# Two heads at a time through TensorE in the attention of the last two mixers

## The reference, cut to what matters

```python
def stick_breaking_attention(q, k, v):          # (heads 8, S = 256, dh = 64)
    z = q @ k.T * dh ** -0.5
    earlier = key_pos < query_pos
    log_keep = where(earlier, log_sigmoid(-z), 0.0)
    log_stick = cumsum(log_keep, over keys, reverse) - log_keep
    w = where(earlier, exp(log_sigmoid(z) + log_stick), 0.0)
    return w @ v
```

## Time and profile before

| what | value |
|---|---|
| median of 3 runs | 2064.53 us (2064.52 to 2066.67) |
| span of the profiled execution | 2064.4 us |
| TensorE matmul busy | 2025.7 us, 98% |
| VectorE busy | 1374.4 us, 67% |
| ScalarE busy | 1105.1 us, 54% |
| mean granted TensorE clock | 0.996 of full speed |

### The profile page before, as it was taken

How to read it: one execution, slowest core, us unless ns; L and a number is a source line. 1 busy time by engine, 2 the same in 40 slices (tenths; PEclk the granted TensorE clock), 3 DMA queues, 4 the chain that set the end, 5 groups by cost and what they waited for, 6 DMA issues and landing times.

```text
span 2064.4 us, 28014 instructions
## 1 busy us (share of the span) xinstructions
PE 2025.7 (98%) x11020; PEld 1705.3 (83%) x11020; DVE 1374.4 (67%) x2469; ACT 1105.1 (54%) x1722; POOL 28.6 (1%) x59
## 2 busy tenths in 40 slices
PE   7999999998989999999999999999999999999998
PEld 5988899987767788888898788888888898788886
DVE  4456566556785557655697888655755787888653
ACT  4345455445554445654646766544654646666542
POOL 0000000000000000000000000000000000000000
PEclk9999999999999999999999999999999999999999
DMA  9786576664355855756534367554765534357551
GB/s 335 257 293 234 175 259 203 210 218 155 105 164 188 261 183 176 230 179 213 191 114 143 123 215 223 184 183 153 227 191 191 199 123 153 120 187 245 184 183 43
DMA packets 281763, 392.94 MB, mean 190 GB/s; under 512 B 9580, under 2 KB 175900, under 8 KB 281504
## 3 DMA queue, kind: packets, MB, share of 16 engines
q1 hardware_dynamic: 277472, 379.62, 56.3%
q0 software_dynamic: 3184, 9.04, 1.4%
q10 hardware_dynamic: 976, 2.49, 0.3%
HBM read 390.06 MB, written 1.05 MB: 189 GB/s over the span
## 4 chain that ended last, share of the span: by engine, by line
PE 67%; DVE 4%; issue 3%; ACT 2%; DMA 1%; POOL 0%; DVEq 0%; SPq 0%; ACTq 0%; POOLq 0%
PE bank L828 18%; PE bank L830 18%; PE bank L829 18%; PE bank L792 10%; PE bank L953 1%; DVE wlo L1982 1%; DMA raw<-in_ffn_w_in 1%; PE bank L876 1%; ACT whi L1395 0%; DVE tm L2803 0%; DVE stats L2057 0%; DVE x L2218 0%; ACT junk L1455 0%; DVE stats L2063 0%; DMA pm<-in_pool 0%
## 5 line engine op out<-in xcount | busy, mean ns | idle before, releaser
L1982 DVE TENSOR_TENSOR wlo<-raw,whi 128x1024 fp32r<-128x1024 f32 x360 | 434.2, 1223 | 312.7 <-ACT whi L1395 311.5
L1395 ACT ACTIVATE whi<-raw 128x1024 fp32r<-128x1024 f32 x360 | 375.1, 1058 | 404.5 <-PE bank L830 208.1
L828 PE MATMUL bank<-whi,xTh 128*128 128x512 f32 (+1 forms) x1344 | 528.5, 393 | 5.2 <-DVE xTl L2046 2.0
L830 PE MATMUL bank<-whi,xTl 128*128 128x512 f32 (+1 forms) x1344 | 521.2, 388 | 0.0
L829 PE MATMUL bank<-wlo,xTh 128*128 128x512 f32 (+1 forms) x1344 | 520.7, 387 | 0.0
L1987 DVE SCALAR_TENSOR_TENSOR wlo<-raw,cols,whi 128x512 fp32r<-128x512 f32 (+2 forms) x608 | 407.1, 723 | 139.6 <-ACT whi L1400 136.0
L1400 ACT ACTIVATE whi<-raw,cols 128x512 fp32r<-128x512 f32 (+2 forms) x608 | 385.7, 696 | 147.0 <-PE bank L830 107.8
L828 PEld LDWEIGHTS bank<-whi,xTh 128*128 128x128 f32 x1344 | 253.0, 188 | 60.7 <-issue 6.8
L830 PEld LDWEIGHTS bank<-whi,xTl 128*128 128x128 f32 x1344 | 252.8, 188 | 52.5
L829 PEld LDWEIGHTS bank<-wlo,xTh 128*128 128x128 f32 x1344 | 253.2, 188 | 48.5
L792 PE MATMUL bank<-xTh,whi 128*128 128x256 f32 x696 | 198.0, 285 | 0.4 <-DVE wlo L1982 0.4
(11 more groups left out here) (364 smaller groups left out, 2473.7 us busy)
## 6 DMA issues: line engine op xcount, KB each, us to landing
raw<-in_w_in SPq DMA_DIRECT2D x68, 1024.0 KB, 5.2
raw<-in_ffn_w_in SPq DMA_DIRECT2D x132, 512.0 KB, 6.2
raw<-in_ffn_w_gate SPq DMA_DIRECT2D x88, 512.0 KB, 4.1
raw<-in_ffn_w_up SPq DMA_DIRECT2D x88, 512.0 KB, 5.1
raw<-in_ffn_w_down SPq DMA_DIRECT2D x40, 1024.0 KB, 5.0
raw<-in_w_mod SPq DMA_DIRECT2D x36, 1024.0 KB, 5.8
raw<-in_ffn_w_out SPq DMA_DIRECT2D x30, 1024.0 KB, 5.2
raw<-in_w_out SPq DMA_DIRECT2D x12, 1024.0 KB, 5.1
```

Source lines behind the costliest of these rows:

```text
L828: e.matmul(o, hi[:, kc, sl], wh[:, c], start=at == 0 and k == 0, stop=False)
L830: ins = e.matmul(o, lo[:, kc, sl], wh[:, c], start=False, stop=fin)
L1395: e.activation(wh, raw, ACT.Copy).then_inc(m.whi_done, 1)
L1982: e.tensor_tensor(wl, raw, wh.bitcast(F32), ALU.subtract).then_inc(m.wlo_done, 1)
```

## The change

The two heads of a pair (2p, 2p+1) are now issued together, alternating between the two halves of the array. `scores(p)` runs in steps 0, 2, 4, 6 for two heads and takes two banks; `values(p)` runs in steps 3, 5, 7, 9 for two heads; `sticks` stays one head a step. The running sums take a product of 384 columns and one of 128 instead of one of 256 and two of 128. ScalarE keeps its order, head by head; `ex` has three buffers (`h % 3`), and ScalarE's waits for the values change with it. The tables of banks and of weights are untouched.

```diff
-        self.ex, o = self.at(o, "ex", [128, 2, 384])
+        self.ex, o = self.at(o, "ex", [128, 3, 384])
...
-        def values(h):
-            hp, off, r = h // 2, (h % 2) * 64, h % 2
-            pr = slice(off, off + 64)
-            self.evacuated("sc", l, h)
...
-            self.mm(bank[pr, cs:cs + 256], m.sv[:, 0, hc], m.ex[:, r, 0:256], h % 4 < 2, False)
-            ins = self.mm(bank[pr, cs + 128:cs + 256], m.sv[:, 1, hc], m.ex[:, r, 256:384], False, h % 4 >= 2)
-            ins.then_inc(m.full[b] if h % 4 == 3 else m.value_mm, 1)
+        def values(p):
+            b, _ = self.t.bank["bo", l, p // 2]
+            bank, cs = m.psum[b], p % 2 * 256
+            for h in (2 * p, 2 * p + 1):
+                self.evacuated("sc", l, h)
...
+            for i, n in ((0, 256), (1, 128)):
+                for h in (2 * p, 2 * p + 1):
+                    pr, hc = slice(h % 2 * 64, h % 2 * 64 + 64), slice(h * 64, h * 64 + 64)
+                    ins = self.mm(bank[pr, cs + 256 - n:cs + 256], m.sv[:, i, hc], m.ex[:, h % 3, i * 256:i * 256 + n],
+                                  i == 0 and p % 2 == 0, i == 1 and p % 2 == 1)
+            ins.then_inc(m.full[b] if p % 2 else m.value_mm, 1)
...
-            self.mm(bank[:, 0:256], NL, m.spl[:, r, 0:256], False, False)
-            self.mm(bank[:, 128:256], NO, m.spl[:, r, 256:384], False, False)
-            self.mm(bank[:, 256:384], NL, m.spl[:, r, 256:384], False, True).then_inc(m.stick_mm, 1)
-
-        def scores(h):
...
-            bank, full = self.bank("sc", l, h)
-            self.mm(bank[:, 0:256], m.kT[pr, hp, 0:128], m.qT[pr, hp, 0:256], True, False)
-            self.mm(bank[:, 256:384], m.kT[pr, hp, 128:256], m.qT[pr, hp, 128:256], False, False)
-            o = bank[:, :].rearrange("p (a n) -> p a n", a=2)[:, :, 0:128]
-            self.mm(o, m.one2[:, :], m.maskr[:, :, :], False, False).then_inc(full, 1)
+            self.mm(bank[:, 0:384], NL, m.spl[:, r, :], False, False)
+            self.mm(bank[:, 128:256], NO, m.spl[:, r, 256:384], False, True).then_inc(m.stick_mm, 1)
+
+        def scores(p):
...
+            pair = [self.bank("sc", l, h) for h in (2 * p, 2 * p + 1)]
+            for i, n in ((0, 256), (1, 128)):
+                for x, (bank, _) in enumerate(pair):
+                    pr = slice(64 * x, 64 * x + 64)
+                    self.mm(bank[:, i * 256:i * 256 + n], m.kT[pr, p, i * 128:i * 128 + 128], m.qT[pr, p, 256 - n:256], i == 0, False)
+            for bank, full in pair:
+                o = bank[:, :].rearrange("p (a n) -> p a n", a=2)[:, :, 0:128]
+                self.mm(o, m.one2[:, :], m.maskr[:, :, :], False, False).then_inc(full, 1)
 
         def each():
             n = step[0]
             step[0] += 1
-            if 2 <= n < 10:
-                values(n - 2)
+            if n in (3, 5, 7, 9):
+                values((n - 3) // 2)
             if 1 <= n < 9:
                 sticks(n - 1)
-            if n < 8:
-                scores(n)
+            if n in (0, 2, 4, 6):
+                scores(n // 2)
...
-            x = m.ex[:, h % 2, :]
-            if h == 5:
+            x = m.ex[:, h % 3, :]
+            if h in (5, 6):
                 self.filled("bo", l, 0)
-            elif h >= 2:
-                e.wait_ge(m.value_mm, 6 * l + h - 1 - (h - 2 >= 4))
+            elif h >= 3:
+                e.wait_ge(m.value_mm, 2 * l + 1 + (h == 7))
```

More of the change, by code:

```diff
@@ L1204, in mixer @@
         step = [0]
-        def values(h):
-            hp, off, r = h // 2, (h % 2) * 64, h % 2
-            pr = slice(off, off + 64)
-            self.evacuated("sc", l, h)
-            if h % 4 == 0:
-                self.bank("bo", l, h // 4)
-                if h == 0:
-                    self.evacuated("sv", l, 1)
-            b = self.t.bank["bo", l, h // 4][0]
-            bank, cs, hc = m.psum[b], (hp % 2) * 256, slice(h * 64, h * 64 + 64)
-            self.mm(bank[pr, cs:cs + 256], m.sv[:, 0, hc], m.ex[:, r, 0:256], h % 4 < 2, False)
-            ins = self.mm(bank[pr, cs + 128:cs + 256], m.sv[:, 1, hc], m.ex[:, r, 256:384], False, h % 4 >= 2)
-            ins.then_inc(m.full[b] if h % 4 == 3 else m.value_mm, 1)
+        def values(p):
[3 more added lines that the diff above has]
+                self.evacuated("sc", l, h)
+            if p % 2 == 0:
+                self.bank("bo", l, p // 2)
+                if p == 0:
+                    self.evacuated("sv", l, 1)
+            for i, n in ((0, 256), (1, 128)):
[4 more added lines that the diff above has]
+            ins.then_inc(m.full[b] if p % 2 else m.value_mm, 1)
         def sticks(h):
@@ L1224, in sticks @@
             e.wait_ge(m.spl_done, 8 * l + h + 1)
-            self.mm(bank[:, 0:256], NL, m.spl[:, r, 0:256], False, False)
-            self.mm(bank[:, 128:256], NO, m.spl[:, r, 256:384], False, False)
-            self.mm(bank[:, 256:384], NL, m.spl[:, r, 256:384], False, True).then_inc(m.stick_mm, 1)
-        def scores(h):
-            hp, off = h // 2, (h % 2) * 64
-            pr = slice(off, off + 64)
-            if h == 0:
+            self.mm(bank[:, 0:384], NL, m.spl[:, r, :], False, False)
+            self.mm(bank[:, 128:256], NO, m.spl[:, r, 256:384], False, True).then_inc(m.stick_mm, 1)
+        def scores(p):
+            if p == 0:
                 self.evacuated("sk", l, 1)
                 e.wait_ge(m.mask_done, l + 1)
-            bank, full = self.bank("sc", l, h)
-            self.mm(bank[:, 0:256], m.kT[pr, hp, 0:128], m.qT[pr, hp, 0:256], True, False)
-            self.mm(bank[:, 256:384], m.kT[pr, hp, 128:256], m.qT[pr, hp, 128:256], False, False)
-            o = bank[:, :].rearrange("p (a n) -> p a n", a=2)[:, :, 0:128]
-            self.mm(o, m.one2[:, :], m.maskr[:, :, :], False, False).then_inc(full, 1)
+            pair = [self.bank("sc", l, h) for h in (2 * p, 2 * p + 1)]
[6 more added lines that the diff above has]
+                self.mm(o, m.one2[:, :], m.maskr[:, :, :], False, False).then_inc(full, 1)
         def each():
@@ L1846, in sticks @@
             b, n = self.t.bank["sc", l, h]
-            e.activation(m.ex[:, h % 2, :], m.psum[b][:, 0:384], ACT.Exp).then_inc(m.free[b], 1)
+            e.activation(m.ex[:, h % 3, :], m.psum[b][:, 0:384], ACT.Exp).then_inc(m.free[b], 1)
         def scores(h):
             bank, _ = self.filled("sc", l, h)
-            x = m.ex[:, h % 2, :]
-            if h == 5:
+            x = m.ex[:, h % 3, :]
+            if h in (5, 6):
                 self.filled("bo", l, 0)
-            elif h >= 2:
-                e.wait_ge(m.value_mm, 6 * l + h - 1 - (h - 2 >= 4))
+            elif h >= 3:
+                e.wait_ge(m.value_mm, 2 * l + 1 + (h == 7))
             e.activation(x, bank[:, 0:384], ACT.Abs).then_inc(m.act, 1)
@@ L2696, in scores @@
                 e.wait_ge(m.stick_mm, 8 * l + h - 1)
-            e.scalar_tensor_tensor(out=m.spl[:, h % 2, :], in0=bank[:, 0:384], scalar=0.0, in1=m.ex[:, h % 2, :],
+            e.scalar_tensor_tensor(out=m.spl[:, h % 2, :], in0=bank[:, 0:384], scalar=0.0, in1=m.ex[:, h % 3, :],
                                    op0=ALU.max, op1=ALU.add).then_inc(m.spl_done, 1)
```

## The result

The kernel after takes 2054.87 us (median of 4 runs, 2053.29 to 2056.50); the runs of before beside it have a median of 2065.6. The ratio is 0.9953, 95% interval 0.9941 to 0.9965. A second set of five runs gave 2054.55 us and again 0.9953 (0.994 to 0.9965).

The account below looks back on a forecast made before the run. TensorE, with matmuls in flight 98% of the span, was taken to bound the kernel. Per mixer 7.7 - 3.2 = 4.5 us, rounded to 4.2; twice that from 2064.4 gives 2056.0 us, own range 2055.0 to 2057.6, wide range 2054.5 to 2060.5.

Parts of the forecast that it names:

- Cost of a pair: TensorE, attention: two heads on different halves cost what one did, 0.85 us for scores and 0.80 for values.
- R1: Rival, scores: halves of rows do not overlap, a pair costs 0.85 + 0.64, net 2.4 per mixer, 2059.6 us; chance 0.08.
- no overlap at all: Rival, scores and values: neither halves of rows nor of columns overlap, net 0.5 per mixer, 2063.4 us; chance 0.03.
- R2: Rival, values: halves of columns have weight loads exposed, 8 of 0.05 us per pair, 2057.2 us; chance 0.04.
- R4: Rival, pairs: alternating halves exposes every load without overlap, scores 2.1 us, values 1.7, 2073.4 us in all; chance 0.03.
- The waits: TensorE idles for VectorE's `spl` before the running sums: 1.64, 1.0 and 0.3 us at heads 1, 5 and 7.
- R5: Rival, running sums: the wait on `spl` is larger because ScalarE's ln comes late too, 2059.5 us; chance 0.05.
- gross saving: TensorE per mixer: fewer blocks of scores and values and fewer changes of shape save 7.7 us before losses.
- the rounding of 4.5 to 4.2: Net saving per mixer, 7.7 - 3.2 = 4.5 us, rounded down to 4.2 for unplaced unevenness in the three waits.
- The base: Whole kernel: the saving was taken from the profiled span of 2064.4 us, said to lie 0.1 below the runs' median.
- R3: Rival, clock: TensorE's idle at head 1 brings the 1.2 GHz level, 0.7 to 2.7 us per mixer, 2059.5; chance 0.09.
- The lead behind the attention: Product behind `gate2`: VectorE about 3.4 us earlier and TensorE 4.2, leaving 2 us of cover over the last tap.

Follow-up runs that it names:

- the kernel with one half: The kernel after, with the scores of both heads of a pair contracting over the same lower 64 partitions: 2060.74 us.
- the kernels without the taps: The kernel after, with four of the 31 convolution taps left out in each mixer (two of step 1, two of step 5): 2049.97 us.
- with the taps moved: The kernel after, with three VectorE taps of steps 1 and 5 moved ahead of the attention: 2050.41 us, ratio to before 0.9932.
- the doubled kernel with head after head: The kernel after, with every score product issued twice and one head's products all ahead of the other's: mixers of 58.86 and 62.05 us.

## Why the prediction came out as it did

- **Bound.** That TensorE's own time counts at once until another engine is late: right. 9.25 us came out of the two mixers, and behind them nothing was given back.
- **Cost of a pair.** 0.85 and 0.80 were said, 0.86 and 0.80 measured. R1 (halves of rows one after the other, 1.49) and no overlap at all are out; the kernel with one half shows what R1 would have been: 1.51 and a mixer of 55.9, so R1's 2.4 net per mixer was right within 0.3 (58.61 - 55.92 = 2.7).
- **R2, exposed loads in the values**, the outcome by the rule of the Trainium skill ("TensorE: Matmul & The Clock Gate", "The mechanism") that a load overlaps only another row group: a pair of values costs no more than one head did. The trace disagrees with the rule here.
- **R4, slower.** It supposed that changing halves pass by pass exposes every load, 2.1 a pair; alternating took 0.86. Its price was also summed wrong: by its own costs a mixer takes 4 x (1.25 + 0.90) = 8.6 us more than forecast, not 10.2, so it would have come out about 0.9 slower than before and not 4.5.
- **The waits.** 1.64, 1.0 and 0.3 at heads 1, 5 and 7 were said; 1.53, 0.76 and 0.36 came, in both mixers, at no other heads. The step of the method (TensorE's arrival from starts minus savings, VectorE's readiness from its row of instructions) held; that the first two are VectorE's is shown by the kernels without the taps and with the taps moved, and the third went when VectorE's states were put behind `spl`. R5, ScalarE, is out.
- **The terms.** Without the waits for taps a mixer takes 51.58, less its wait of 0.36: 51.2. So the gross saving is 58.61 - 51.22 = 7.4, said 7.7; and the losses are 54.00 - 51.22 = 2.8, of which 2.65 are waits, said 3.2. The two errors nearly cancel: 4.6 per mixer, where my own sum gave 4.5. Part of the missing 0.3 of gross saving is in step 8: from its first piece to `reads` before takes 4.63 us (1149.14 to 1153.77) and after 3.83 (1141.98 to 1145.81), 0.80 less where 1.0 was said. **The mis-sized step is the rounding of 4.5 to 4.2** "for an unevenness in the three waits that I cannot place"; nothing in the trace stood for it. In two mixers it is 0.6 us of the 0.85 by which the gain was forecast too small (8.4 for 9.25).
- **The base.** I took the span of the profiled execution for the median of runs, which left out 2.2 us between a span and its run, and did not see that this execution was slower than most. With spans alone the forecast was 2064.4 - 8.4, with medians 2064.53 - 8.4: the same number by luck, as the two slips cancel.
- **The range.** The forecast's own range, 2055.0 to 2057.6, was missed by 0.1 and by 0.45 us in the two sets. The lower end of the wide one, 2054.5, was said to stand for waits 2 and 3 absent; by the prediction's own terms that would be 7.7 - 1.64 - 0.1 = 5.96 per mixer, 2052.5. So 2054.5 had no working behind it, and it is luck that it lay just below what came.
- **Two slips without effect.** The attention's part of step 2 is 2.93 us (1111.31 to 1114.24), not 3.02. And the loads: `reads` shows 32 x 64 columns in 1.09 us, 1880 per us, while four loads of 128 in 0.22 are 2330, not "just at that rate". Full overlap was therefore less well supported than it was said to be; the measured 0.86 shows that the loads keep up.
- **R3, the clock.** In after it stayed at 1.00 in both mixers, in two profiles. Rejected for this kernel, but not for its neighbours, as below. Its main row does not carry what was read from it: the idle time of 2.18 us at 475 stands, as 2.18 or 2.19, in all fourteen profiles of this document, and is followed by 0.50 in nine of them and by 1.00 in five, the second profile of after among these.
- **The lead behind the attention.** 2 us of cover over the last tap were said: the tap ends at 1151.2, TensorE comes at 1153.29.

## What to carry to other kernels

Where an operand fills half of the array, issue two such products for different halves close together; in this kernel (plain fp32, 64 rows or 64 columns of the array) the second was free, and the order inside four passes did not matter. Then ask at once which producer on another engine the faster engine now runs into: here two fifths of the gross saving went into waits for it, and three small jobs moved into that producer's idle time brought back 4 us, an edit that was worth nothing before. Before moving work behind a waiting instruction, look at what the engine will do during that wait.

## What the runs showed of the hardware that was not expected

**TensorE starts passes out of the order of issue, with a reach of four.** Four passes of one half ahead of four of the other cost the same as alternating (0.86 a block); eight ahead of eight cost 2.26, and the ninth pass starts beside the fifth. Whether the four are passes, or two fp32 products of two passes each, no run here tells apart.

**The same wait was followed by the lower clock once in twelve.** Waits for `spl` of 1.48 to 1.53 us stand at head 1 in both mixers of six profiles. Eleven were followed by 1.00. After the twelfth, in the second mixer of the doubled kernel with head after head, windows of 2 us show (columns as above):

```profile
1734.00:1736.00 2.00, 0.57 (x3) 0.15 (x1) 2.00 (x6) 1.05 (x2) 0.00 (x0) 1.00 0.00 0
1736.00:1738.00 2.00, 1.95 (x10) 1.51 (x12) 2.00 (x4) 0.49 (x1) 0.00 (x0) 1.00 0.00 0
1738.00:1740.00 2.00, 2.00 (x11) 1.87 (x10) 2.00 (x7) 0.00 (x0) 0.00 (x0) 0.51 0.67 179
1740.00:1742.00 2.00, 2.00 (x7) 1.59 (x6) 0.48 (x2) 0.74 (x2) 0.00 (x0) 0.50 0.89 345
1742.00:1744.00 2.00, 2.00 (x6) 1.55 (x5) 0.56 (x1) 1.97 (x4) 0.00 (x0) 0.50 0.00 0
```

TensorE was idle 1.48 us up to 1736.05, worked two more microseconds at full clock (1.06 us of running sums on the whole array, then the first scores, on half of its rows), and then ran at 0.50 (1.2 GHz) for nearly 7 us. The mixer took 62.05 us, its twin with the same wait 58.86: 3.2 us. Why this one and not the eleven others stays open; the price is above the 0.7 to 2.7 us per mixer that R3 gave. So the level behind an idle time of this length could not be told in advance from one profile, and a wait of 1.5 us may cost more than its own length.
